# The first modulation's order, loads by row pieces, and half of the later modulations summed on VectorE

## What is computed

```python
c_act = jax.nn.silu(c)
mod = jnp.einsum('bd,dm->bm', c_act, w_ada[l]) + b_ada[l]
shift_m, scale_m, gate_m, shift_f, scale_f, gate_f = jnp.split(mod, N_MOD, axis=-1)
h = modulate(rms_norm(x, g_norm_mix[l]), shift_m, scale_m)      # h * (1 + scale) + shift
p = jnp.einsum('bsd,dk->bsk', h, w_in[l])                       # 1024 -> 512 + 5 * 1024
...
y = jnp.einsum('becf,efd->becd', jax.nn.silu(a) * u, w_down_e)  # 16 experts, 2048 wide
```

## Time and profile before

| | |
|---|---|
| runs, median (lowest to highest) | 1314.11 us (1312.86 to 1314.63), 3 runs |
| the profiled execution, its time / its span | 1314.88 / 1313.1 us |
| busy PE / DVE / ACT / POOL | 75% / 29% / 19% / 2% of the span |
| chain that ended last | DMA 56%, PE 42% |
| read from memory | 494.71 MB, mean 378 GB/s |

### The profile page before, as it was taken

The page is one execution under the profiler, slowest core; times in us unless marked ns, Lnnn a source line. Parts: engine busy times, 40 slices in busy tenths (PEclk is TensorE's granted clock), DMA queues, the critical chain, the costliest instruction groups (busy, mean ns, idle before and its releaser), DMA issues.

```text
span 1313.1 us, 15613 instructions
## 1 busy us (share of the span) xinstructions
PE 979.5 (75%) x6766; PEld 559.6 (43%) x6766; DVE 378.1 (29%) x575; ACT 247.5 (19%) x375; POOL 21.6 (2%) x47
## 2 busy tenths in 40 slices
PE   8999999878665665655656655657556666899998
PEld 7999998323121221212121221212121221478988
DVE  4698866210000110000010100000010100388865
ACT  4453434001000000000000000000000000467744
POOL 2000200000000000000000000000000000000000
PEclk8999999988787888689798878888786887999999
DMA  9998999899999999999999999999999999965230
GB/s 336 389 377 311 321 389 414 351 430 430 427 434 428 431 431 431 426 434 433 431 431 431 426 431 437 431 430 431 429 427 436 429 430 421 392 234 161 97 128 33
DMA packets 70156, 496.43 MB, mean 378 GB/s; under 512 B 4794, under 2 KB 26954, under 8 KB 49632
## 3 DMA queue, kind: packets, MB, share of 16 engines
q1 hardware_dynamic: 67792, 489.11, 90.4%
q0 software_dynamic: 2080, 6.55, 1.5%
q10 hardware_dynamic: 240, 0.11, 0.0%
HBM read 494.71 MB, written 1.06 MB: 378 GB/s over the span
## 4 chain that ended last, share of the span: by engine, by line
DMA 56%; PE 42%; DVE 1%; issue 1%; ACT 0%; ACTq 0%; SPq 0%; DVEq 0%
DMA ring<-in_w_down_e 23%; DMA ring<-in_w_up_e 18%; DMA ring<-in_w_gate_e 15%; PE psum L734 8%; PE psum L735 8%; PE psum L736 8%; PE psum L1142 7%; PE psum L1169 4%; PE psum L1180 1%; PE psum L885 1%; PE psum L1222 1%; PE psum L1077 0%; DMA arena<-in_b_ada 0%; PE psum L797 0%; PE psum L1257 0%
## 5 line engine op out<-in xcount | busy, mean ns | idle before, releaser
L1142 PE MATMUL psum<-ring,arena 128*32 128x512 f32 x2048 | 304.2, 743 | 192.8 <-DMA ring<-in_w_up_e 111.6
L1169 PE MATMUL psum<-ring,arena 128*32 128x512 f32 x976 | 162.2, 800 | 98.1 <-DMA ring<-in_w_down_e 97.5
L1142 PEld LDWEIGHTS psum<-ring,arena 128*32 128x32 f32 x2048 | 70.8, 130 | 385.8 <-issue 179.0
L1169 PEld LDWEIGHTS psum<-ring,arena 128*32 128x32 f32 x976 | 42.8, 137 | 203.9 <-issue 143.7
L1763 DVE TENSOR_TENSOR ring_r<-ring,ring_r 128x2048 fp32r<-128x2048 f32 x49 | 111.1, 2289 | 36.6 <-ACT ring_r L1380 36.4
L1540 ACT ACTIVATE arena<-psum 128x512 f32<-128x512 f32 x16 | 9.6, 598 | 535.2 <-PE psum L1142 535.2
L734 PE MATMUL psum<-ht_hi,ring_r 128*128 128x256 f32 x384 | 109.5, 285 | 0.0
L735 PE MATMUL psum<-ht_lo,ring_r 128*128 128x256 f32 x384 | 108.1, 281 | 0.0
L736 PE MATMUL psum<-ht_hi,ring_r 128*128 128x256 f32 x384 | 107.6, 280 | 0.0
L2081 DVE TENSOR_TENSOR arena<-psum,arena 128x512 f32<-128x512 f32 x32 | 20.6, 686 | 290.0 <-PE psum L1169 290.0
L1380 ACT ACTIVATE ring_r<-ring 128x2048 fp32r<-128x2048 f32 x49 | 92.4, 1910 | 29.2 <-PE psum L736 24.1
(11 more groups left out here) (291 smaller groups left out, 921.8 us busy)
## 6 DMA issues: line engine op xcount, KB each, us to landing
ring<-in_w_gate_e SPq DMA_DIRECT2D x23, 4096.0 KB, 33.4
ring<-in_w_up_e SPq DMA_DIRECT2D x22, 4096.0 KB, 33.0
ring<-in_w_down_e SPq DMA_DIRECT2D x21, 4096.0 KB, 33.8
ring<-in_w_up_e SPq DMA_DIRECT2D x16, 2048.0 KB, 36.5
ring<-in_w_in SPq DMA_DIRECT2D x31, 1024.0 KB, 9.7
ring<-in_w_gate_e SPq DMA_DIRECT2D x14, 2048.0 KB, 36.2
ring<-in_w_down_e SPq DMA_DIRECT2D x14, 2048.0 KB, 36.9
ring<-in_w_ada SPq DMA_DIRECT2D x16, 1024.0 KB, 10.3
```

The source lines that it names most:

```text
L1142: last = mm(psum[32 * g:32 * g + 32, b, :].rearrange("s (q c) -> s q c", c=4), cur[h][:, k, :], w[:, g // 2, :, g % 2 * 4:g % 2 * 4 + 4], ...
L1169: last = mm(psum[32 * q:32 * q + 32, 2 + n, :], act_t[:, f % 4, (f // 4) * CAP:(f // 4 + 1) * CAP], w[:, kk, n * BANK:(n + 1) * BANK], sta ...
```

## The change

It has four parts.

1. **Step 0's modulation and x's quarters.** PE computes k 0 to 3 as soon as c is ready, before quarter 0, k 4 and 5 behind quarter 0, k 6 and 7 behind quarter 1, then quarter 2 and `turn_step(0)`. Quarter 3 and the late vectors move behind the row products of step 0. Two of the six fillers go. ACT's copies of quarters 1 to 3 move behind its splits of v0 and c0.
2. **Loads by row pieces.** The second modulation slot of step 0 comes in two k and two k (four loads of 256 KB for two of 512), and step 0's half of fourier_in in one k and one k (two for one). ACT and DVE split it by k, in turn with `step_hi` and `step_lo`; this raises the counts of `first_hi` and `first_lo` by one, and all later waits on them.
3. **VectorE sums the first slot** of the modulation of steps 1 to 3 (`sum_half`): w[k] = w[k] * c[k] + w[k - 1] over four k, in place. PE (`later_modulation`) uses the second slot's 16 matmuls, then 4 with weights of ones on the sum, in place of 16; both slots are released at its end. In step 0 it stands behind the first piece of c0, and `turn_step(1)` behind the second.
4. **Semaphores merged:** the loads of p and w_pp count on one, those of g_final and the bias on another.

```diff
@@ load_modulation / load_opening (SP) @@
-                for part in range(2):
-                    sp.dma_start(slot_in(s, k=FG, part=2, n=STEP_K * P)[:, :, part, :], head_stream[s][:, :, part, :]).then_inc(loaded[place(s)], 16)
+                if s == mod_slots[0][1]:
+                    for rows, done in ((slice(0, 2), front_mod_loaded), (slice(2, FG), loaded[place(s)])):
+                        for part in range(2):
+                            sp.dma_start(slot_in(s, k=FG, part=2, n=STEP_K * P)[:, rows, part, :], head_stream[s][:, rows, part, :]).then_inc(done, 16)
...
+                if st == 0 and name == "fourier_in":
+                    sp.dma_start(slot_in(s, k=FG, n=BANK)[:, 0:1, :], head_stream[s][:, 0:1, :]).then_inc(front_row_loaded, 16)
+                    rows = slice(1, STEP_K)
...
@@ PE @@
+            def later_modulation(st):
+
+                first, second = mod_slots[st]
+                to = [psum[32 * g:32 * g + 32, 6, st % 2 * P:(st % 2 + 1) * P] for g in range(4)]
+                arrived(pe, second)
+                w = slot_in(second, k=FG, n=BANK)
+                for kk in range(FG):
+                    for g in range(4):
+                        mm(to[g], c_rep[:, FG + kk, :], w[:, kk, g * P:(g + 1) * P], start=(kk == 0), stop=False, tile_position=(0, 32 * g))
+                pe.wait_ge(half_summed, st)
+                summed = slot_in(first, k=FG, n=BANK)[:, FG - 1, :]
+                for g in range(4):
+                    last = mm(to[g], ones[:, 0:32], summed[:, g * P:(g + 1) * P], start=False, stop=True, tile_position=(0, 32 * g))
+                last.then_inc(slot_used, 2)
...
             for st in range(STEPS):
                 opening_rows(st)
                 if st == 0:
+                    turn_quarter(xr, 3, 5)
+                    turn_late_vectors()
                     pe.wait_ge(raw_kept, 2)
                 opening_columns(st, "v0")
                 if st == 0:
                     pe.wait_ge(raw_kept, 4)
+                    opening_columns(st, "c0", pieces=(0,))
+                    later_modulation(st + 1)
+                    opening_columns(st, "c0", lambda: turn_step(st + 1), pieces=(1, 2, 3))
+                    continue
...
@@ ACT, step 0 @@
             keep_raw(0, 0)
+            keep_step(0)
+            for k in range(STEP_K):
+                split_first(k)
+                step_hi(0, (k,))
+            split_opening(0, "v0")
             keep_raw(1, 1)
+            split_opening(0, "c0")
             keep_raw(2, 4)
-            keep_step(0)
-            split_opening(0, "fourier_in")
-            step_hi(0)
-            split_opening(0, "v0")
             keep_raw(3, 5)
-            split_opening(0, "c0")
@@ DVE @@
+            def sum_half(st):
+
+                s = mod_slots[st][0]
+                arrived(dve, s)
+                w = slot_in(s, k=FG, n=BANK)
+                link(V.tensor_scalar(w[:, 0, :], w[:, 0, :], c_act[:, 0:1], None, ALU.mult))
+                for k in range(1, FG):
+                    ins = V.scalar_tensor_tensor(w[:, k, :], w[:, k, :], c_act[:, k:k + 1], w[:, k - 1, :], ALU.mult, ALU.add)
+                    if k < FG - 1:
+                        link(ins)
+                ins.then_inc(half_summed, 1)
...
             late_columns()
+            sum_half(1)
             for st in range(1, STEPS):
...
                 split_opening(st, "c0")
+                if st + 1 < STEPS:
+                    sum_half(st + 1)
```

More of the change, by code:

```diff
@@ L801, in opening_rows, with opening_columns @@
                     last.then_inc(slot_used, 1)
[L803 to L805 removed]
+            def opening_columns(st, name, between=None, pieces=range(4)):
+                pe.wait_ge(first_lo, 1 + len(OPENING) * st + OPENING.index(name) + 1)
                 w = opening_slot(st, name)
@@ L808, in opening_columns @@
                     for c in range(2):
+                        if 2 * j + c not in pieces:
+                            continue
                         at = slice((2 * j + c) * P, (2 * j + c + 1) * P)
@@ L812, in opening_columns @@
                                                  (ht_hi[:, k, :], ht_lo[:, k, :]), k == 0 and c == 0, k == KD - 1 and c == 1)
-                        if j == 0 and c == 0 and between:
+                        if between and 2 * j + c == pieces[0]:
                             between()
@@ L874, in sum_partitions, with first_modulation @@
                 last.then_inc(ada_summed, 1)
[L876 to L880, removed]
-                    w = slot_in(s, k=FG, n=BANK)
[L882 to L887, removed]
+            def first_modulation(ks):
+                for k in ks:
+                    half, kk = divmod(k, FG)
+                    s = mod_slots[0][half]
+                    if k == FG:
+                        pe.wait_ge(front_mod_loaded, 32)
+                    elif k in (0, FG + 2):
+                        arrived(pe, s)
+                    w = slot_in(s, k=FG, n=BANK)
+                    for g in range(4):
+                        last = mm(psum[32 * g:32 * g + 32, 6, 0:P], c_rep[:, k, :], w[:, kk, g * P:(g + 1) * P],
+                                  start=(k == 0), stop=(k == KD - 1), tile_position=(0, 32 * g))
+                    if kk == FG - 1:
+                        last.then_inc(slot_used, 1)
+            def later_modulation(st):
[8 more added lines that the diff above has]
+                summed = slot_in(first, k=FG, n=BANK)[:, FG - 1, :]
+                for g in range(4):
+                    last = mm(to[g], ones[:, 0:32], summed[:, g * P:(g + 1) * P], start=False, stop=True, tile_position=(0, 32 * g))
+                last.then_inc(slot_used, 2)
             def turn_step(st):
@@ L1417, in weigh_ada, with split_first @@
                 f(w, w, ACT.Copy, scale=c_act[:, k:k + 1]).then_inc(ada_weighted, 1)
+            def split_first(k):
+                s = unit_slots["fourier_in"][0]
+                cols = slice(k * BANK, (k + 1) * BANK)
+                act.wait_ge(opening_loaded["fourier_in"] if k else front_row_loaded, 16)
+                f(ring_r[part_place[s]][:, cols], ring[:, place(s), cols], ACT.Copy).then_inc(first_hi, 1)
             def split_opening(st, name):
```

84 lines of the change are left out of this document (51 added, 33 removed).

## The result

| | before | after |
|---|---|---|
| median (lowest to highest), 4 runs each | 1313.54 us (1312.86 to 1314.63) | 1322.63 us (1321.5 to 1323.0) |
| after / before | | 1.0065, 95% interval 1.0053 to 1.0078 |
| profiled execution, time / span | 1314.88 / 1313.1 us | 1322.75 / 1321.0 us |
| VectorE's accumulation of the last expert, where the tail begins | 1132.57 us | 1131.36 us |
| from there to the end of the span | 180.5 us | 189.6 us |

By the medians the change makes the kernel 9.1 us slower, outside the range forecast. By the two profiled executions it is 7.9, since the one of before was 1.3 us above its median: the last 190 us lose 9.1, and the tail begins 1.2 us earlier.

A forecast was written before the change was run, and what follows sets the result against it. The experts' DMA load stream was taken to bound the kernel after its last dry spell, ending at 238.72 us; an earlier opening gains one to one. Gain 1.03 less 0.24 made 0.8 us: 1313.3 us, 8-in-10 range 1311.6 to 1315.1.

The forecast's parts named there:

- The step that failed: From 60 us on: merged semaphores (p with w_pp, g_final with bias) wait for landings long over, so they cost nothing.
- The landings of v0, through ScalarE's copy, set the turns: Opening, steps 2 and 3: row turns at 37.95 and 48.02, fixed by landings, not TensorE; third turn 1.03 us earlier.
- The copy: ScalarE's copy of step 2's modulation row follows its v0 split directly, at 37.6, and takes 0.28 us.
- TensorE's own saving: Modulation of steps 1 to 3: 40 records, 1.18 us for 1.89, so 0.71 us less per step, 2.13 in all.
- VectorE's sum: Opening, steps 1 to 3: scaling and three multiply-adds take about 2.8 us in VectorE's idle time, ending before TensorE asks.
- The pieces: Opening's load queue: three extra loads for the same bytes delay the landings by 0.24 us, bounds nothing and 0.5.
- (d): Load queue: each piece costs some 2 us, landings come 6 us later, kernel slower at 1319.1 us; chance 0.02.
- The carry: From 60 us on: the opening's 0.8 us gain reaches the issue ending the dry queue at 238.72, and the end.
- The sum: Opening's gain of 1.03 us less 0.24 for the extra loads: 0.8 us, median 1313.3 us.
- (a): Opening: TensorE's whole saving arrives, the turn not binding; gain 2.3 to 3.0 us, 1311.8 to 1311.1; chance 0.13.
- (b): Nothing arrives: extra loads cost 0.3 each, or a split in the last opening step or near 110 is late; 1314.1; chance 0.12.
- (c): Step 2's turn: TensorE's 1.15 us pause halves its clock for some 6.8 us, kernel slower at 1316.7; chance 0.05.

The follow-up runs named there:

- run 2: The kernel before with one edit, final gain and bias counted on one semaphore, both VectorE waits asking for 32: 1323.3 us, ratio 1.0072.
- run 1: The changed kernel with the final gain counted with p and w_pp, and the bias alone on the other count: 1312.65 us, ratio 0.9988.
- run 3: The changed kernel with only the first half of the bias loaded, the wait as it is: 1318.32 us, ratio 1.0029.
- run 4: The changed kernel with VectorE's split of k_diff's second half written ahead of the wait for gain and bias: 1320.59 us, ratio 1.0055.
- run 6: run 1's kernel with step 0's two loads (second modulation half and fourier_in) undivided again: 1312.59 us, ratio 0.9989.
- run 7: The kernel before with one edit, VectorE summing the first half of the modulation of steps 1 to 3: 1312.2 us, ratio 0.9987.
- run 5: run 1's kernel with TensorE, not VectorE, summing both halves of the later steps' modulation: 1314.8 us, ratio 1.0003.
- run 8: run 1's kernel with 36 idle products (8.2 us of filler) on TensorE between the opening and the head: 1320.75 us.

## Why the prediction was wrong

**The step that failed** is one sentence: the merged semaphores (p with w_pp, g_final with bias) "wait for landings that are long over". For p, w_pp and g_final that holds. For the bias it does not, and with it falls the premise at the head of the prediction, that all that the change does to the time lies before 60 us. The term was put at nothing without a row. The trace of before had it. GpSimd issues the bias behind the count of q_diff's slot, at 1142.88, since the bias goes into a slot of the ring. Its row there says when it is there (of the answer on the tensor in_bias, before):

```profile
DMA to landing us min/median/max: 13.6/13.6/13.6
```

That is 1156.5, and VectorE's gain started at 1147.32. A wait for the later of two landings had to stand for 9.2 us. What the runs showed in place of nothing is 9.61 us on VectorE, 6.33 on TensorE and 2.1 through the clock, some 9 us in all; run 2 has it alone (ratio 1.0072), and run 1, without it, is back under before. The rows that price it are the timeline of VectorE in the tail and the one above. I had looked at the waits as counts, not at who waits on each. There are two waiters on `side_loaded`: `score_rows`, which needs the bias and comes late (1177.19 in before), and the gain, which needs only g_final and now gets the condition of the other. Merging counts that are waited for in two places is adding a wait, and it was to be costed like one, with what is queued behind it on VectorE (the split of k_diff's second half, the norms, q_dil's splits) and who waits for that (TensorE, with 3.0 us to spare before: the split ended at 1152.4, and TensorE had the first half's products until 1155.4, which is the 1154.2 of after and the 1.2 by which its tail begins earlier). None of the four rivals had this place.

The Trainium skill, "DMA: Bandwidth & Descriptors", section "Why a DMA increments its semaphore by 16 and not by 1", asks for one semaphore for each slot in flight, because a wait for the first of two loads on one count can pass before it has landed. After has one count for two loads, and avoids an early pass by waiting for the sum of both, 32. That such a wait can pass too early, no run here shows. The traces show the other side of it: the price of waiting for both is the landing of the later load.

**What held.**

- *The landings of v0, through ScalarE's copy, set the turns.* The turn of step 2 was to wait for ScalarE's copy of the row, bound by v0's landing, at 37.95 and 0.24 for the pieces; it started at 37.73. TensorE's waiting there was to be about 1.1 us. In after it was only 0.11, but with the same opening it was 0.53 in run 1, 1.20 in run 3 and 1.15 in run 4, with the turn at 37.71 to 37.79 each time: when TensorE comes earlier it waits longer, and the turn stays. The third turn was to be at 48.02 and 0.24; it is at 47.75:

```profile
36.45 1.06 ACT L1477 ACTIVATE ring_r<-ring 128x1024 fp32r<-128x1024 f32 x1 [0.30 <-DMA ring<-in_w_in]
...
37.42 0.26 ACT L1484 ACTIVATE arena<-psum 128x128 f32<-128x128 f32 x1
...
47.44 0.26 ACT L1484 ACTIVATE arena<-psum 128x128 f32<-128x128 f32 x1
```

```profile
35.42 1.08 PE L917 MATMUL psum<-ring,arena 128*32 128x128 f32 x32
36.32 0.40 PE L921 MATMUL psum<-ring,arena 128*32 128x128 f32 x8
...
37.73 0.33 PE L927 MATMUL psum<-arena 128*128 128x128 f32 x1
...
47.75 0.33 PE L927 MATMUL psum<-arena 128*128 128x128 f32 x1
```

  and the turn of step 2 in run 4, which has the same opening:

```profile
37.71 0.33 PE L927 MATMUL psum<-arena 128*128 128x128 f32 x1 [1.15 <-ACT arena L1484]
```

- *The copy.* 37.42 where I had 37.6: the split started at 36.45 and not 36.53, and the copy began 0.97 behind the split's start and not 1.06, since durations on ScalarE overlap a little. With a copy of 0.26 for 0.28 these make the 0.2 us by which the turns are earlier than forecast before the 0.24 for the pieces; the rest is that the pieces did not cost their 0.24.
- *TensorE's own saving* was taken a little too large. The 40 records of a later modulation take 0.90 (35.42 to 36.32) and 0.33 (36.32 to 36.65, the next product), 1.23 in all, for 1.18 forecast. In step 0 the first product of v0 was to start at 21.65, and started at 22.23 in after; the spread there (20.97 to 22.23 with the same opening) holds both, so the forecast of step 0 is neither borne out nor refuted.
- *VectorE's sum* was to take 2.8 us, from 32.5 to 35.3:

```profile
32.81 0.48 DVE L1933 TENSOR_SCALAR ring<-ring,arena 128x512 f32<-128x512 f32 x1
33.33 2.33 DVE L1935 SCALAR_TENSOR_TENSOR ring<-ring,arena 128x512 f32<-128x512 f32 x3
```

  32.81 to 35.66, 2.85 us, and no wait of TensorE on it in any step of after. The bound by the nearest row (0.69 us for a two-input operation) was good: the three of them take 0.78 each with their handoffs.
- *The pieces* were to delay the landings by 0.24 us. Run 6 has v0's landing wait of step 2 end at 36.37, run 1 at 36.45: 0.08. That is no more than the spread from trace to trace: without pieces this wait ends between 36.35 and 36.53 (before and runs 2, 6, 7), with them between 36.44 and 36.71 (after and runs 1, 3, 4, 5, 8). So rival (d), 6 us, is refuted. The Trainium skill, same page, section "Anatomy of one DMA", gives a fixed cost of about 2.0 us for each DMA, fitted on the software path; three of them would make 6 us, an estimate from that page. The runs here show none of it, for loads of the SP queue that stand behind others.
- *The carry* from the opening to the end, one to one through the issue that ends the dry stretch, is what run 8 shows for a delay of 8.2 us (8.1 at the end). For the gain, after issues it at 236.94 for 238.72; forecast was 237.9. But in runs 1, 6 and 7, with the third turn within 0.1 us, this issue is at 238.14, 236.66 and 237.69: a single profile can't tell less than 1.5 us here, as the spell at half clock between 223 and 240 us lies elsewhere in each (the clock is 0.57 in 225 to 230 in before, and 0.52 in 235 to 240 in after). Over all traces it points the right way: 236.63 to 238.14 in the six with VectorE's sum and no filler, and 238.18 to 239.92 in the three without the sum.
- *The sum* of the opening, 0.8 us: run 1 has 1.0 us by medians and 1.6 by the ratio (0.4 to 2.8). Apart from the merged count, 1313.3 was within a microsecond of the 1312.65 measured. The interval is too wide to tell 0.8 from twice as much.

**The rivals.** (a) more of the saving arrives: its condition, that the turn doesn't bind, is refuted by the turns, since that of step 3 stays at 47.68 to 47.93 in all seven traces with the sum (TensorE's whole saving would have put it near 46.9, 49.05 less 2.13, an estimate). The times alone don't tell it from the forecast. (b) nothing arrives: excluded by runs 1, 6 and 7, narrowly. (c) the clock: in 25 to 60 us of after it stays at 1.00 with TensorE busy 34.89 of 35. After is a weak test, as its pause was 0.11 us; but in runs 3 and 4 the pause was 1.20 and 1.15 us, as long as forecast, and the clock stayed at 1.00 there too. So (c) is refuted at its own place. But the mechanism was real and struck where I hadn't looked, behind the 6.33 us wait in the tail, for 2.1 us. (d): above.

## What to carry to other kernels

Before two loads share a count, list every wait on either, and give each the landing of the later load as its new condition: the price is that landing less the time at which the earlier waiter now passes, both in the trace, and what is queued behind the waiter. Merge loads with the same waiters or landings close together; here g_final fitted with p and w_pp, and cost nothing. And a part of a change that saves no time by itself is still to be followed through the whole program: this one stood 1100 us away from everything else that was edited.

## What the runs showed of the hardware

- TensorE's clock fell to 1.2 GHz during a wait of 6.33 us (after), 5.60 (run 2) and 5.62 (run 4), and came back after 4.3, 2.8 and 5.2 us of work. In two runs it fell in a place where no single wait was over 1.5 us: in run 3 among waits of 0.85, 1.47 and 1.18 us in 1171.9 to 1177.4, and in run 2 a second time at 1182.8, in the last of waits of 0.53, 0.76 and 1.37 us in 1178.5 to 1183.0. The same place with two waits, of 0.53 and 0.97 us (before, run 1) or 0.53 and 1.37 (after), kept 2.4 GHz.
- Two loads from two queues share the engines: the bias, 3 MB issued by GpSimd beside loads of 1 MB from SP, took 14.1 us in after (13.4 to 14.4 in the nine traces that load it whole), and half of it 9.0.
- Three extra loads in a queue with a backlog moved later landings by 0.08 us in all (run 1 against run 6), less than the 0.2 to 0.3 us by which traces of kernels with the same loads differ.
